# An expert's rows gathered from DRAM by an indirect DMA in place of one-hot matmuls

## The chip, the cores and the metric

The kernel runs on one core of one Trainium2 chip. The metric is the device time of one execution in microseconds, lower is better. TensorE (PE) multiplies, VectorE (DVE) and ScalarE (ACT) do elementwise work, GpSimd (POOL) has a queue of its own for transfers, and SyncE (SP) issues the weight transfers. All transfers of the core share its 16 DMA engines.

## What is computed

A two-layer encoder on 256 tokens of 1024 channels in float32. Each layer adds a mixer (attention, Fourier and recurrent branches) and a feed-forward block. The block of the second layer is the one that matters here, a mixture of 8 experts of which each token uses 2:

```
logits = xt @ w_router                      # (256, 8)
top_v, top_i = top_k(logits, 2)
top_w = softmax(top_v)
comb = sum(one_hot(top_i, 8) * top_w[..., None], axis=1)
for e in range(8):
    y = y + comb[:, e:e+1] * swiglu(xt, w_gu[e], w_down[e])
```

`xt` is the normalized input of the block. The expert widths are 1024 to 2 x 1536 and 1536 to 1024.

## The kernel before

**Precision.** Matmuls on fp32r operands stand in for float32 ones: each operand is split into a high part (`_hi`, an ACT copy that rounds) and a low part (`_lo`, a DVE subtraction), and three matmuls (high x high, high x low, low x high; L1245 to L1247) make one product.

**Weights.** They come in units of 128 x 1024 floats (512 KB). SP issues one transfer for each, and in the experts a ring of 18 units is filled ahead: unit u is issued when DVE has split unit u-18. ACT (L456) and DVE (L758) split each unit into a ring of four, and ACT may start unit u only when PE has used unit u-4. In the code of ACT and DVE, step k of a turn splits unit k, three ahead of PE (`AHEAD = 3`).

**An expert's turn.** The loop runs over the 8 experts, 36 units each. Only the tokens routed to an expert are computed: up to 128 slots, which is one tile. A second pass `experts(1)` for more than 128 tokens stands behind a condition and is not executed with these inputs. DVE builds `g_t`, a one-hot matrix of tokens against slots (`build_g`, L1078). PE multiplies it by the normalized activations, which were split once into `yhf` and `ylf` (`gather`, L1470 and L1471: 8 matmuls of 128x512). ACT and DVE copy the two halves of the result from PSUM into `xrow` (L654, L1105). PE transposes `xrow` (`turn_rows`, L1481: 8 transposes), and ACT and DVE split the result into `xg_h` and `xg_l` (L659, L1110), on which the gate and up matmuls of the next turn run. So the rows of expert e+1 are gathered within turn e, between units 24 and 25, and turned between units 27 and 28. The results of an expert are put back by `scatter` (L1491, L1492) with the transposed one-hot matrix `gt_t`, and DVE adds them to `h` (L1124).

**PE's order in a turn:** gate and up units 0 to 7, `scatter` of the last expert, units 8 to 15 with `turn_product(0)` (L1556) between, transposes of `g_t` and a matmul for the slots' weights (L1577, L1579), down units 16 to 19, `turn_product(1)`, gate and up units 20 to 24, `gather`, units 25 to 27, `turn_rows`, down units 28 and 29, `turn_product(2)`, 30 to 35.

**Ahead of the turns.** After the norm (L769), PE transposes the activations (L1306). ACT and DVE copy the result (L683, L1130) and split the normalized rows (L679, L1135, and L435 on POOL). The router's matmuls (L1501) and a chain of small DVE steps (L1189 to L1207) give each token's place. DVE builds the first `g_t`; PE gathers and turns the first rows. `keep_warm(n)` (L1295) is n transposes whose result nobody reads.

**The table `cst`** holds constants; **`hn`** is the part of `gates` that holds the normalized rows.

Of the kernel before, what the change touches and what calls it, by code (L numbers as in the profile page):

```python
# [8 lines left out]
F32 = mybir.dt.float32  # L9
F32R = mybir.dt.float32r  # L10
# [56 lines left out]
NA = len(UNITS_ATT)  # L67


C_ID, C_TRI, C_ONE, C_IOTA, C_CC, C_MASK, C_DFT, C_I8 = 0, 128, 256, 384, 640, 896, 960, 1472  # L70
C_COLS = 1480
FIRST_SLOTS = 128


def constants():

    c = np.zeros((P, C_COLS), np.float32)
    i = np.arange(P)
    c[:, C_ID:C_ID + P] = np.eye(P)
    c[:, C_TRI:C_TRI + P] = i[:, None] < i[None, :]  # L80
    c[:, C_ONE:C_ONE + P] = 1.0
    c[:, C_IOTA:C_IOTA + P] = np.where(i < FIRST_SLOTS, i, -1)
    c[:, C_IOTA + P:C_IOTA + 2 * P] = FIRST_SLOTS + i
# [16 lines left out]
    c[:, C_I8:C_I8 + 8] = np.arange(8)  # L100
    return c


def build(nc, x, norm_mix_g, w_in, b_in, rpb, conv_w, conv_b, lru_wa, lru_ba, lru_wx, lru_bx,
# [12 lines left out]
    with ExitStack() as ctx:  # L117
# [3 lines left out]
        def sem(name):  # L121
# [43 lines left out]
        gt_t = sb("gt_t", [P, TT, P], F32R)  # L165
        idx = sb("idx", [P, TT, 8], U32)
        cnt_i = sb("cnt_i", [P, 2], I32)
        eps_t = sb("eps_t", [P, 1])
        ps = ctx.enter_context(nc.psum_tensor("ps", [P, 8, 512], F32))

# [68 lines left out]
        hnh_ok, hnl_dve, hnl_pool, xt_a, xt_d, lg_ps, lg_row, lg_t, lg_d, w2_ok, mask_ok, comb_ok, pos_ps, cnt_ps, cnt_ok = (  # L239
            sem("hnh_ok"), sem("hnl_dve"), sem("hnl_pool"), sem("xt_a"), sem("xt_d"), sem("lg_ps"), sem("lg_row"), sem("lg_t"), sem("lg_d"), sem("w2_ok"), sem("mask_ok"), sem("comb_ok"), sem("pos_ps"),  # L240
            sem("cnt_ps"), sem("cnt_ok"))
        g_ok, gr_ps, xr_a, xr_d, gth_ps, xgh_ok, xgl_ok, gt_ps, gt_ok, slot_zero, ysh_ok, ysl_ok, sc_ps, sc_add = (
            sem("g_ok"), sem("gr_ps"), sem("xr_a"), sem("xr_d"), sem("gth_ps"), sem("xgh_ok"), sem("xgl_ok"), sem("gt_ps"), sem("gt_ok"), sem("slot_zero"),
            sem("ysh_ok"), sem("ysl_ok"), sem("sc_ps"), sem("sc_add"))
# [160 lines left out]
        def _(pool):  # L405
# [25 lines left out]
            mixer(1)  # L431
            load_row(final_g, 0, normed, 2 * TT * 4)

            pool.wait_ge(hnh_ok, 1)
            pool.tensor_tensor(ylf[:, 0:D], gflat[:, 0:D], yhf[:, 0:D].bitcast(F32),  # L435
                               ALU.subtract).then_inc(hnl_pool, 1)


        @block.scalar
        def _(act):  # L440
# [203 lines left out]
            def experts(p):  # L644
# [29 lines left out]

                if p == 0:

                    for t in range(TT):
                        act.wait_ge(normed, 2 * (TT * 3 + t + 1))
                        act.activation(yhf[:, D * t:D * t + D], gflat[:, D * t:D * t + D], ACT.Copy).then_inc(hnh_ok, 1)  # L679
                        if t == 0:  # L680
                            for b in range(2):
                                act.wait_ge(xt_ps, 4 * 3 + b + 1)
                                act.activation(xt_full[:, 512 * b:512 * b + 512], ps[:, 4 + b, :],  # L683
                                               ACT.Copy).then_inc(xt_a, 1)
# [6 lines left out]
                else:  # L691
                    for k in range(AHEAD):
# [3 lines left out]
                gather_rows((E + 1) * p, 0)  # L696
                gather_hi((E + 1) * p, 0)
                act.wait_ge(slot_zero, p + 1)
                def turn(e, last):

                    rows_hi((E + 1) * p + 1, e)
                    for k in range(AHEAD, U_EX + AHEAD):
                        if k < U_EX or not last:
                            hi(B, k, e, U_EX)
                        if k == 4 + AHEAD:
                            silu(e, 0)
                        if k == 11 + AHEAD:
                            product_hi(e, 0)
                        if k == 12 + AHEAD:
                            silu(e, 1)  # L710
                        if k == 16 + AHEAD:
                            act.wait_ge(gt_ps, e + (E * p + 1))
                            act.activation(gt_t[:, :, :].rearrange("p t s -> p (t s)"), ps[:, 6, 0:2 * P], ACT.Copy)\
                               .then_inc(gt_ok, 1)
                            act.activation(slot_w, ps[:, 6, 2 * P:2 * P + 1], ACT.Copy).then_inc(gt_ok, 1)
                        if k == 20 + AHEAD:
                            product_hi(e, 1)
                        if k == 24 + AHEAD:
                            silu(e, 2)
                        if k == 25 + AHEAD:  # L720
# [24 lines left out]
        def _(dve):  # L745
# [337 lines left out]
            def experts(p):  # L1083
# [13 lines left out]
                def product_lo(s, e):  # L1097
# [29 lines left out]
                if p == 0:  # L1127
                    for b in range(2):
# [9 lines left out]
                    route()  # L1138
                build_g(p, 0)
                if p == 0:  # L1140
                    route_weights()
# [4 lines left out]
                gather_rows((E + 1) * p, 0)  # L1146
                gather_lo((E + 1) * p, 0)
                def turn(e, last):

                    rows_lo((E + 1) * p + 1, e)  # L1150
                    for k in range(AHEAD, U_EX + AHEAD):
# [23 lines left out]
                        if k == 33:  # L1175
                            product_lo(2, e)
# [63 lines left out]
        def _(pe):  # L1240
# [192 lines left out]
            def dense():  # L1433
# [27 lines left out]
                    down(B + 28, 2, False, False, i, 12)  # L1461
                down(B + U_FF - 4, FF_STEPS, False, True, c=BC)

            def gather(n, e):

                pe.wait_ge(g_ok, e + n)
                for half in range(2):
                    for t in range(TT):
                        o = D * t + 512 * half
# [1 line left out]
                        ins = mm(ps[:, 6 + half, :], g_t[:, t, :], ylf[:, o:o + 512], start=False, stop=(t == TT - 1))  # L1471
                    ins.then_inc(gr_ps, 1)

            def turn_rows(n, e):

                for c in range(KC):
                    if c == 0:
                        pe.wait_ge(xr_a, e + n)
                    if c == KC // 2:
# [38 lines left out]
            def experts(p):  # L1518
                B = BASE_MOE + p * E * U_EX
                n0 = (E + 1) * p  # L1520
                if p == 0:
                    pe.wait_ge(hnl_dve, 1)
                    pe.wait_ge(hnl_pool, 1)
                    keep_warm(5)
                gather(n0 + 1, 0)
                if p == 0:
                    keep_warm(3)
                turn_rows(n0 + 1, 0)
                if p == 0:
                    keep_warm(6)  # L1530

# [36 lines left out]
                with pe.Fori(0, E) as e:  # L1568
# [64 lines left out]
```

## Time and profile before

| | |
|---|---|
| median of three runs | 1172.76 us (1170.49 to 1172.87) |
| the profiled execution | 1171.27 us, with a span of 1169.5 us from the first instruction to the last |
| mean granted TensorE clock | 0.991 |
| TensorE busy | 1133.6 us, 97% of the span |
| VectorE busy | 877.4 us, 75% |
| ScalarE busy | 720.5 us, 62% |
| GpSimd busy | 24.9 us, 2% |
| DMA | 271.70 MB, mean 232 GB/s |

A row of a group of instructions gives line, engine, operation, the tiles written and read, shapes and count, then busy time and the mean of one in ns, then idle time of the engine before them. Matmuls overlap, so the distance from one start to the next, and not the duration of one, is what a matmul costs PE. The granted clock is 1.00 at 2.4 GHz, and 0.5 stands for the lower level, 1.2 GHz. The DMA share is the busy share of the 16 engines; transfers that overlap in an engine bring it a little over 1.

### The profile page before, as it was taken

The numbers are of one execution on the slowest core, as the hardware profiler recorded it, in microseconds if no ns is written. First come the engines' busy times: TensorE is split into PE (matmuls) and PEld (weight loads), VectorE is DVE, ScalarE is ACT, GpSimd is POOL, SyncE is SP. The second block draws the span as 40 slices with busy tenths as digits, with TensorE's granted clock in tenths as the row PEclk, the third lists the DMA queues.
The fourth block names the chain that finished last, engine by engine and source line by source line (L and its number), as shares of the span: only waits on it lengthen the run. The fifth ranks groups of instructions, "written<-read, shape, count | busy, mean of one in ns | idle before, by whom it ended". The sixth has DMA issues, their size and how long they took to land.

```text
span 1169.5 us, 19502 instructions
## 1 busy us (share of the span) xinstructions
PE 1133.6 (97%) x7004; PEld 996.7 (85%) x7004; DVE 877.4 (75%) x1049; ACT 720.5 (62%) x941; POOL 24.9 (2%) x21
## 2 busy tenths in 40 slices
PE   7999999989999998999999989999999999999995
PEld 7989899889999997989899868888888888888883
DVE  5976876755445456765886779999999999998995
ACT  5476764454443445376764457778787877777773
POOL 0200000000000001200000000000000000000000
PEclk9999999999999999999999999999999999999998
DMA  9954455646555567655445398999999999999940
GB/s 291 261 178 148 126 168 167 205 147 190 187 183 178 165 211 206 189 158 158 136 151 174 112 374 301 343 331 330 341 327 341 326 342 325 344 326 345 329 139 38
DMA packets 137897, 271.70 MB, mean 232 GB/s; under 512 B 26424, under 2 KB 26736, under 8 KB 137840
## 3 DMA queue, kind: packets, MB, share of 16 engines
q1 hardware_dynamic: 136832, 267.26, 69.4%
q0 software_dynamic: 1008, 3.67, 0.9%
q8 instruction: 37, 0.61, 0.2%
q14 instruction: 20, 0.16, 0.1%
HBM read 269.84 MB, written 1.05 MB: 232 GB/s over the span
## 4 chain that ended last, share of the span: by engine, by line
PE 82%; DVE 9%; ACT 5%; issue 3%; DMA 1%; DVEq 0%; ACTq 0%; POOLq 0%
PE ps L1245 25%; PE ps L1247 24%; PE ps L1246 24%; DVE w_lo L758 4%; ACT w_hi L456 2%; DVE h L1124 2%; PE ps L1358 1%; PE ps L1306 1%; PE ps L1491 1%; PE ps L1492 1%; PE ps L1471 1%; PE ps L1470 1%; PE ps L1386 1%; PE ps L1332 1%; PE ps L1481 1%
## 5 line engine op out<-in xcount | busy, mean ns | idle before, releaser
L758 DVE TENSOR_TENSOR w_lo<-raw,w_hi 128x1024 fp32r<-128x1024 f32 x304 | 370.3, 1232 | 177.6 <-ACT w_hi L456 172.7
L456 ACT ACTIVATE w_hi<-raw 128x1024 fp32r<-128x1024 f32 x304 | 318.0, 1060 | 218.0 <-PE ps L1247 208.1
L1245 PE MATMUL ps<-xh,w_hi 128*128 128x256 f32 x1024 | 292.3, 285 | 0.4 <-DVE xl L779 0.4
L1247 PE MATMUL ps<-xh,w_lo 128*128 128x256 f32 x1024 | 289.7, 283 | 0.0
L1246 PE MATMUL ps<-xl,w_hi 128*128 128x256 f32 x1024 | 289.7, 283 | 0.0
L758 DVE TENSOR_TENSOR w_lo<-mix,w_hi 128x1024 fp32r<-128x1024 f32 x192 | 230.4, 1220 | 29.1 <-ACT w_hi L456 24.0
L456 ACT ACTIVATE w_hi<-mix 128x1024 fp32r<-128x1024 f32 x192 | 203.7, 1061 | 71.9 <-PE ps L1247 71.9
L1245 PE MATMUL ps<-w_hi,xh 128*128 128x512 f32 x512 | 203.3, 397 | 0.8 <-issue 0.2
L1247 PE MATMUL ps<-w_hi,xl 128*128 128x512 f32 x512 | 199.8, 390 | 0.0
L1246 PE MATMUL ps<-w_lo,xh 128*128 128x512 f32 x512 | 199.4, 389 | 0.0
L1245 PEld LDWEIGHTS ps<-xh,w_hi 128*128 128x128 f32 x1024 | 196.4, 192 | 3.1 <-issue 2.1
L1246 PEld LDWEIGHTS ps<-xl,w_hi 128*128 128x128 f32 x1024 | 196.4, 192 | 0.3
L1247 PEld LDWEIGHTS ps<-xh,w_lo 128*128 128x128 f32 x1024 | 196.3, 192 | 0.0
L1245 PEld LDWEIGHTS ps<-w_hi,xh 128*128 128x128 f32 x512 | 96.3, 188 | 26.0 <-DVE w_lo L758 5.9
L1245 PE MATMUL ps<-w_hi,yh 128*128 128x512 f32 x288 | 115.4, 401 | 0.8
L1247 PEld LDWEIGHTS ps<-w_hi,xl 128*128 128x128 f32 x512 | 96.1, 188 | 20.8
L1247 PE MATMUL ps<-w_hi,yl 128*128 128x512 f32 x288 | 112.5, 391 | 0.0
L1246 PEld LDWEIGHTS ps<-w_lo,xh 128*128 128x128 f32 x512 | 96.3, 188 | 18.9
L1246 PE MATMUL ps<-w_lo,yh 128*128 128x512 f32 x288 | 112.3, 390 | 0.0
L1245 PEld LDWEIGHTS ps<-w_hi,yh 128*128 128x128 f32 x288 | 54.1, 188 | 14.2 <-issue 4.1
L1247 PEld LDWEIGHTS ps<-w_hi,yl 128*128 128x128 f32 x288 | 54.1, 188 | 11.8
L1246 PEld LDWEIGHTS ps<-w_lo,yh 128*128 128x128 f32 x288 | 54.2, 188 | 10.2
(202 smaller groups left out, 1126.6 us busy)
## 6 DMA issues: line engine op xcount, KB each, us to landing
mix<-in_moe_w_gu_dram SPq DMA_DIRECT2D x112, 512.0 KB, 5.2
raw<-in_w_in_dram SPq DMA_DIRECT2D x96, 512.0 KB, 4.2
raw<-in_moe_w_gu_dram SPq DMA_DIRECT2D x80, 512.0 KB, 5.6
mix<-in_moe_w_down_dram SPq DMA_DIRECT2D x80, 512.0 KB, 4.6
raw<-in_ffn_w_gu_dram SPq DMA_DIRECT2D x48, 512.0 KB, 3.8
raw<-in_w_branch_dram SPq DMA_DIRECT2D x24, 512.0 KB, 3.4
raw<-in_ffn_w_down_dram SPq DMA_DIRECT2D x24, 512.0 KB, 4.7
raw<-in_w_out_dram SPq DMA_DIRECT2D x16, 512.0 KB, 3.4
```

The source lines that it names most:

```text
L456: act.activation(w_hi[:, u % RH, :], src, ACT.Copy).then_inc(hi_done, 1)
L758: dve.tensor_tensor(w_lo[:, u % RH, :], place(u)[0], w_hi[:, u % RH, :].bitcast(F32), ALU.subtract).then_inc(lo_done, 1)
L1124: dve.tensor_tensor(h[:, t, 512 * half:512 * half + 512], ps[:, (6, 7, 4, 5)[q], :], h[:, t, 512 * half:512 * half + 512], ALU.add).then_i ...
L1245: mm(dst, ah, bh, start=first, stop=False, skip_group_check=True)
L1246: mm(dst, ah, bl, start=False, stop=False, skip_group_check=True)
L1247: return mm(dst, al, bh, start=False, stop=last, skip_group_check=True)
L1306: ins = pe.transpose(ps[:, 4 + c // 2, at:at + P], hn[:, t, P * c:P * c + P], ident)
L1332: ins = mm(ps[:, 4 + m, 0:SEQ], uf_t[:, BR * t + P * m:BR * t + P * m + P], cst[:, at:at + SEQ], start=(t == 0), stop=(t == TT - 1))
L1358: ins = mm(ps[q, 4 + 2 * g + m // 2, SEQ * (m % 2):SEQ * (m % 2) + SEQ], wlru[q, d, g, m, :], conv_t[q, m, :], start=True, stop=True)
L1386: ins = mm(ps[HD * hh:HD * hh + HD, 6, P * t:P * t + P], v_t[:, kt, HD * hd:HD * hd + HD], pt_t[:, hh, P * kt:P * kt + P], start=(kt == 0) ...
L1470: mm(ps[:, 6 + half, :], g_t[:, t, :], yhf[:, o:o + 512], start=(t == 0), stop=False)
L1471: ins = mm(ps[:, 6 + half, :], g_t[:, t, :], ylf[:, o:o + 512], start=False, stop=(t == TT - 1))
```

## The change

The normalized rows are written once to a DRAM tensor `hn_rows` (two POOL transfers of 512 KB). For each expert PE multiplies `g_t` by the tokens' numbers (`token_id`, two equal columns), which gives the row number of each slot; DVE casts one column to `slot_row`, and POOL issues an indirect DMA that fetches row `slot_row[p]` of `hn_rows` into partition p of `xrow` (128 rows of 4 KB). Empty slots fetch row 0. In the first pass the splits of the normalized rows, the one-hot matmuls and the two copies into `xrow` are gone. In the second pass, which isn't executed, they stand as before. On PE the row numbers are computed between units 23 and 24, and the rows are turned between units 29 and 30. `build_g` moves from step 23 to step 21 of DVE, `gather_hi` and `gather_lo` from steps 31 to 32.

```
# POOL
-            pool.wait_ge(hnh_ok, 1)
-            pool.tensor_tensor(ylf[:, 0:D], gflat[:, 0:D], yhf[:, 0:D].bitcast(F32),
-                               ALU.subtract).then_inc(hnl_pool, 1)
+            for t in range(TT):
+                pool.wait_ge(normed, 2 * (TT * 3 + t + 1))
+                pool.dma_start(hn_rows[P * t:P * t + P, :], hn[:, t, :]).then_inc(rows_out, 16)
+
+            def gather_rows():
+
+                pool.indirect_dma_start(xrow, None, hn_rows, bass.IndirectOffsetOnAxis(slot_row[:, 0:1], 0)).then_inc(xr_in, 16)
+
+            pool.wait_ge(rows_out, 16 * TT)
+            pool.wait_ge(row_ok, 1)
+            gather_rows()
+            for e in range(E):
+
+                pool.wait_ge(row_ok, e + 2)
+                pool.wait_ge(gth_ps, 2 * e + 2)
+                gather_rows()
# ACT, ahead of the turns: the copies of hn into yhf go; in a turn gather_rows only if p
-                    for t in range(TT):
-                        act.wait_ge(normed, 2 * (TT * 3 + t + 1))
-                        act.activation(yhf[:, D * t:D * t + D], gflat[:, D * t:D * t + D], ACT.Copy).then_inc(hnh_ok, 1)
...
-                        if k == 25 + AHEAD:
-                            gather_rows((E + 1) * p + 1, e)
-                        if k == 28 + AHEAD:
+                        if p and k == 25 + AHEAD:
+                            gather_rows(1, e)
+                        if k == 29 + AHEAD:
                             gather_hi((E + 1) * p + 1, e)
# DVE
+                def rows_of_slots(n, e=0):
+                    dve.wait_ge(row_ps, e + (n + 1))
+                    dve.tensor_copy(slot_row[:, :], ps[:, 7, 0:1]).then_inc(row_ok, 1)
...
-                    dve.wait_ge(hnh_ok, 2)
-                    dve.tensor_tensor(ylf[:, D:2 * D], gflat[:, D:2 * D], yhf[:, D:2 * D].bitcast(F32),
-                                      ALU.subtract).then_inc(hnl_dve, 1)
...
-                        if k == 23:
+                        if k == 21:
 
                             dve.wait_ge(gt_ps, e + (E * p + 1))
                             build_g(p, e + 1)
+                        if k == 23:
                             product_lo(1, e)
-                        if k == 28:
-                            gather_rows((E + 1) * p + 1, e)
-                        if k == 31:
+                        if p == 0 and k == 26:
+                            rows_of_slots(1, e)
+                        if p and k == 28:
+                            gather_rows(1, e)
+                        if k == 32:
                             gather_lo((E + 1) * p + 1, e)
# PE
+            def rows_of_slots(n, e):
+
+                pe.wait_ge(g_ok, e + n)
+                for t in range(TT):
+                    ins = mm(ps[:, 7, 0:2], g_t[:, t, :], token_id[:, t, :], start=(t == 0), stop=(t == TT - 1))
+                ins.then_inc(row_ps, 1)
...
-            def turn_rows(n, e):
-
+            def turn_rows(n, e, p):
+
+                if p == 0:
+                    pe.wait_ge(xr_in, e * 16 + 16 * n)
...
                 if p == 0:
-                    pe.wait_ge(hnl_dve, 1)
-                    pe.wait_ge(hnl_pool, 1)
-                    keep_warm(5)
-                gather(n0 + 1, 0)
-                if p == 0:
-                    keep_warm(3)
-                turn_rows(n0 + 1, 0)
+                    pe.wait_ge(token_ok, 1)
+                    rows_of_slots(1, 0)
+                    keep_warm(20)
+                else:
+                    pe.wait_ge(hnl_dve, TT)
+                    gather(1, 0)
+                turn_rows(1, 0, p)
...
-                    gate_up(20, 2, e, range(5))
+                    gate_up(20, 2, e, range(4))
                     pe.wait_ge(gt_ok, e * 2 + 2 * (E * p + 1))
-                    gather(n0 + 2, e)
-                    gate_up(20, 2, e, range(5, 8))
-                    turn_rows(n0 + 2, e)
+                    if p:
+                        gather(2, e)
+                    else:
+                        rows_of_slots(2, e)
+                    gate_up(20, 2, e, range(4, 8))
                     down(28, 1, e, range(2))
+                    turn_rows(2, e, p)
                     turn_product(2, e)
```

## Rows read from the trace of the kernel before

**Rows 1.** The page: busy time of each engine.
```profile
PE 1133.6 (97%) x7004; PEld 996.7 (85%) x7004; DVE 877.4 (75%) x1049; ACT 720.5 (62%) x941; POOL 24.9 (2%) x21
```

**Rows 2.** Stretches (a turn; its dense part): PE, PEld, DVE, ACT, POOL, clock, DMA share, GB/s.
```profile
882.40:939.10 56.70, 56.53 (x260) 45.95 (x259) 51.99 (x53) 43.49 (x49) 0.00 (x0) 1.00 0.96 333
905.00:913.50 8.50, 8.50 (x43) 7.08 (x42) 6.67 (x7) 5.98 (x7) 0.00 (x0) 1.00 1.02 373
```

**Rows 3.** Who waited for whom, 769.0 to 1109.1 us (six turns).
```profile
ACT w_hi L456 <- PE ps L1247: 77.4, 174, 2.2
DVE w_lo L758 <- ACT w_hi L456: 21.2, 26, 1.4
PEld ps L1245 <- DVE w_lo L758: 4.4, 12, 0.5
```

**Rows 4.** PE in order of time, one turn: last matmul of unit 23 to turn_rows.
```profile
904.86 0.39 PE L1247 MATMUL ps<-w_hi,xl 128*128 128x512 f32 x1
...
906.45 0.39 PE L1470 MATMUL ps<-yh,g_t 128*128 128x512 f32 x1
...
908.32 0.40 PE L1245 MATMUL ps<-w_hi,xh 128*128 128x512 f32 x1
...
912.43 1.03 PE L1481 MATMUL ps<-cst,gates 128*128 128x128 f32 x8
```

**Rows 5.** PE in order of time: small matmuls in a turn and in the router.
```profile
893.21 0.50 PE L1579 MATMUL ps<-small,g_t 128*128 x4
...
691.34 0.37 PE L1514 MATMUL ps<-small,cst 128*128 128x8 f32 x2
691.56 0.37 PE L1515 MATMUL ps<-small,cst 128*128 128x8 f32 x2
```

**Rows 6.** DVE in order of time, the same turn, and the cast nearest to slot_row.
```profile
902.72 4.90 DVE L758 TENSOR_TENSOR w_lo<-mix,w_hi 128x1024 fp32r<-128x1024 f32 x4
...
911.00 2.59 DVE L758 TENSOR_TENSOR w_lo<-mix,w_hi 128x1024 fp32r<-128x1024 f32 x2 [1.35 <-ACT w_hi L456]
...
691.75 0.17 DVE L1207 COPY small<-ps 128x16 f32<-128x16 f32 x1 [0.85 <-PE ps L1514]
```

**Rows 7.** DMA issues of stretches at 242, 522, 682, 905 us, and of the page: us to landing.
```profile
row<-in_norm_mix_g_dram POOLq DMA_DIRECT2D x1, 512.0 KB, 3.6
...
row<-in_norm_ffn_g_dram POOLq DMA_DIRECT2D x1, 512.0 KB, 7.1
raw<-in_w_in_dram SPq DMA_DIRECT2D x1, 512.0 KB, 6.8
...
row<-in_final_g_dram POOLq DMA_DIRECT2D x1, 512.0 KB, 8.0
...
mix<-in_moe_w_gu_dram SPq DMA_DIRECT2D x5, 512.0 KB, 5.0
...
raw<-in_w_branch_dram SPq DMA_DIRECT2D x24, 512.0 KB, 3.4
```

**Rows 8.** POOL's queue in the microsecond from 686.2: packets, MB, share of 16 engines.
```profile
q0 software_dynamic: 60, 0.25, 62.5%
```

**Rows 9.** Stretches ahead of the turns (columns as in Rows 2).
```profile
676.60:679.70 3.10, 0.59 (x3) 0.17 (x1) 2.75 (x6) 2.42 (x5) 0.00 (x0) 1.00 1.02 385
679.70:683.30 3.60, 3.53 (x17) 3.08 (x18) 2.52 (x6) 2.64 (x6) 1.08 (x2) 0.53 1.04 391
...
700.00:704.00 4.00, 4.00 (x19) 3.31 (x18) 3.90 (x5) 3.53 (x5) 0.00 (x0) 1.00 0.30 57
```

**Rows 10.** Ahead of the turns in order of time: POOL, ACT, DVE, PE.
```profile
682.20 0.53 POOL L410 DMA_DIRECT2D row<-in_final_g_dram  x1 [158.99 <-DVE gates L769]
...
683.06 1.06 ACT L679 ACTIVATE yh<-gates 128x1024 fp32r<-128x1024 f32 x1
...
691.96 0.60 DVE L1078 TENSOR_SCALAR g_t<-cst,small 128x128 fp32r<-128x128 f32 x2
...
698.22 0.48 PE L1245 MATMUL ps<-w_hi,xh 128*128 128x512 f32 x1
```

More of the change, by code:

```diff
@@ L67 @@
 NA = len(UNITS_ATT)
-C_ID, C_TRI, C_ONE, C_IOTA, C_CC, C_MASK, C_DFT, C_I8 = 0, 128, 256, 384, 640, 896, 960, 1472
-C_COLS = 1480
+C_ID, C_TRI, C_ONE, C_IOTA, C_CC, C_MASK, C_DFT, C_I8, C_TOK = 0, 128, 256, 384, 640, 896, 960, 1472, 1480
+C_COLS = 1484
 FIRST_SLOTS = 128
@@ L100, in constants @@
     c[:, C_I8:C_I8 + 8] = np.arange(8)
+    for t in range(TT):
+        c[:, C_TOK + 2 * t:C_TOK + 2 * t + 2] = (t * P + i)[:, None]
     return c
@@ L167, in build @@
         cnt_i = sb("cnt_i", [P, 2], I32)
+        token_id = sb("token_id", [P, TT, 2], F32R)
+        slot_row = sb("slot_row", [P, 1], U32)
+        hn_rows = nc.dram_tensor("hn_rows", (SEQ, D), F32, kind="Internal").ap()
         eps_t = sb("eps_t", [P, 1])
@@ L237, in build @@
         silu_ok, prod_ok, ah_ok, al_ok, at_ps = sem("silu_ok"), sem("prod_ok"), sem("ah_ok"), sem("al_ok"), sem("at_ps")
-        hnh_ok, hnl_dve, hnl_pool, xt_a, xt_d, lg_ps, lg_row, lg_t, lg_d, w2_ok, mask_ok, comb_ok, pos_ps, cnt_ps, cnt_ok = (
-            sem("hnh_ok"), sem("hnl_dve"), sem("hnl_pool"), sem("xt_a"), sem("xt_d"), sem("lg_ps"), sem("lg_row"), sem("lg_t"), sem("lg_d"), sem("w2_ok"), sem("mask_ok"), sem("comb_ok"), sem("pos_ps"),
+        hnh_ok, hnl_dve, xt_a, xt_d, lg_ps, lg_row, lg_t, lg_d, w2_ok, mask_ok, comb_ok, pos_ps, cnt_ps, cnt_ok = (
+            sem("hnh_ok"), sem("hnl_dve"), sem("xt_a"), sem("xt_d"), sem("lg_ps"), sem("lg_row"), sem("lg_t"), sem("lg_d"), sem("w2_ok"), sem("mask_ok"), sem("comb_ok"), sem("pos_ps"),
             sem("cnt_ps"), sem("cnt_ok"))
+        rows_out, token_ok, row_ps, row_ok, xr_in = sem("rows_out"), sem("token_ok"), sem("row_ps"), sem("row_ok"), sem("xr_in")
         g_ok, gr_ps, xr_a, xr_d, gth_ps, xgh_ok, xgl_ok, gt_ps, gt_ok, slot_zero, ysh_ok, ysl_ok, sc_ps, sc_add = (
@@ L675, in experts @@
                 if p == 0:
-                    for t in range(TT):
-                        act.wait_ge(normed, 2 * (TT * 3 + t + 1))
-                        act.activation(yhf[:, D * t:D * t + D], gflat[:, D * t:D * t + D], ACT.Copy).then_inc(hnh_ok, 1)
[L680 to L684, printed above, removed]
+                    for b in range(2):
+                        act.wait_ge(xt_ps, 4 * 3 + b + 1)
+                        act.activation(xt_full[:, 512 * b:512 * b + 512], ps[:, 4 + b, :], ACT.Copy).then_inc(xt_a, 1)
                     link(act.activation(table_in, eps_t[:, 0:1], ACT.Exp))
@@ L691, in experts @@
                 else:
+                    for t in range(TT):
+                        act.activation(yhf[:, D * t:D * t + D], gflat[:, D * t:D * t + D], ACT.Copy).then_inc(hnh_ok, 1)
                     for k in range(AHEAD):
@@ L695, in experts @@
                     link(act.activation(table_in, eps_t[:, 0:1], ACT.Silu))
-                gather_rows((E + 1) * p, 0)
+                else:
+                    gather_rows(0, 0)
                 gather_hi((E + 1) * p, 0)
@@ L1133, in experts @@
                     link(dve.memset(gt_t[:, :, :].bitcast(F32), 0.0))
-                    dve.wait_ge(hnh_ok, 2)
-                    dve.tensor_tensor(ylf[:, D:2 * D], gflat[:, D:2 * D], yhf[:, D:2 * D].bitcast(F32),
-                                      ALU.subtract).then_inc(hnl_dve, 1)
+                    dve.tensor_copy(token_id[:, :, :], cst[:, C_TOK:C_TOK + 2 * TT].rearrange("p (t a) -> p t a", t=TT))\
+                        .then_inc(token_ok, 1)
                     lo(B, 0)
                     route()
+                else:
+                    for t in range(TT):
+                        dve.wait_ge(hnh_ok, t + 1)
+                        dve.tensor_tensor(ylf[:, D * t:D * t + D], gflat[:, D * t:D * t + D],
+                                          yhf[:, D * t:D * t + D].bitcast(F32), ALU.subtract).then_inc(hnl_dve, 1)
                 build_g(p, 0)
                 if p == 0:
+                    rows_of_slots(0)
                     route_weights()
@@ L1145, in experts @@
                     lo(B, k)
-                gather_rows((E + 1) * p, 0)
+                if p:
+                    gather_rows(0, 0)
                 gather_lo((E + 1) * p, 0)
@@ L1462, in dense @@
                 down(B + U_FF - 4, FF_STEPS, False, True, c=BC)
+            def rows_of_slots(n, e):
+                pe.wait_ge(g_ok, e + n)
+                for t in range(TT):
+                    ins = mm(ps[:, 7, 0:2], g_t[:, t, :], token_id[:, t, :], start=(t == 0), stop=(t == TT - 1))
+                ins.then_inc(row_ps, 1)
             def gather(n, e):
-                pe.wait_ge(g_ok, e + n)
+                pe.wait_ge(g_ok, e + (E + 1 + n))
                 for half in range(2):
@@ L1472, in gather @@
                     ins.then_inc(gr_ps, 1)
-            def turn_rows(n, e):
+            def turn_rows(n, e, p):
+                if p == 0:
+                    pe.wait_ge(xr_in, e * 16 + 16 * n)
                 for c in range(KC):
-                    if c == 0:
+                    if p and c == 0:
                         pe.wait_ge(xr_a, e + n)
-                    if c == KC // 2:
+                    if p and c == KC // 2:
                         pe.wait_ge(xr_d, e + n)
@@ L1583, in experts @@
                     turn_product(1, e)
-                    gate_up(20, 2, e, range(5))
+                    gate_up(20, 2, e, range(4))
                     pe.wait_ge(gt_ok, e * 2 + 2 * (E * p + 1))
-                    gather(n0 + 2, e)
-                    gate_up(20, 2, e, range(5, 8))
-                    turn_rows(n0 + 2, e)
+                    if p:
+                        gather(2, e)
+                    else:
+                        rows_of_slots(2, e)
+                    gate_up(20, 2, e, range(4, 8))
                     down(28, 1, e, range(2))
+                    turn_rows(2, e, p)
                     turn_product(2, e)
```

1 line of the change is left out of this document (added).

## The prediction

> **What bounds the kernel now.** I read the page first, then the table of stretches, then the waits, then single turns in order of time. PE is busy for 97% of the span, DVE for 75% [rows 1]. A turn of an expert takes 56.7 us; in it PE is busy 56.53, DVE 51.99 and ACT 43.49 us at a DMA share of 0.96 and 333 GB/s [rows 2]. So three resources are close together, and the waits tell which of them leads. Over six turns ACT waited 77.4 us for PE to free a slot of the weight ring, DVE waited 21.2 us for ACT, and PE waited 4.4 us for DVE [rows 3]. PE sets the pace and pulls the others behind it. The weights come 18 units ahead. With 391 GB/s seen ahead of the turns [rows 9], a turn's 18.9 MB need 48 us, so DMA has slack on the average. It has none in the dense part, with a share of 1.02 at 373 GB/s [rows 2].
>
> **Part 1: what leaves a turn.** From the first gather matmul at 906.45 to unit 25 at 908.32 are 1.87 us [rows 4]. PE has no wait there, so this is its full price. DVE loses one copy of 128x512 from PSUM, and ACT another, some 0.7 us each by the width of a split of twice the size [rows 6]. Neither leads; I count them at nothing. PE covers them, and if that cover were gone they would be worth at most 0.7 us a turn.
>
> **Part 2: what PE gets.** Two matmuls of two columns. No row shows that shape. The nearest are four small ones in a turn, 0.50 us in all (0.25 for two), and the router's, 0.22 us from one pair to the next, which would be 0.45 for two that overlapped no better than those pairs [rows 5]. I take 0.40, near the upper end because the weight loads of `g_t` are alone there. The net gain of PE is 1.87 - 0.40 = 1.47 us a turn, 11.8 us in eight.
>
> **Part 3: the new wait in a turn.** PE waits for `xr_in` ahead of `turn_rows`. Everything is queued behind that on PE, so a late transfer costs its full lateness. Call X the start of unit 23's last matmul, 904.86 in the turn of [rows 4]. The row numbers' second matmul starts at about X+0.4, and 0.41 us pass between such a matmul and the DVE step on it (691.34 to 691.75 [rows 5, 6]), so DVE could cast at X+0.84. But the cast stands behind the split of unit 26. DVE did four splits in 4.90 us from 902.72 [rows 6]; the third of them, unit 26, ended at about 906.4, X+1.5. With 0.17 for the cast and 0.15 for the semaphore POOL issues at X+1.85. PE meanwhile starts unit 24 at X+0.63. Three units take 908.32 to 912.43, 1.37 us each [rows 4]; six of them bring it to `turn_rows` at X+8.8. So the transfer is hidden if it lands within L = 8.8 - 1.85 - 0.1 = 6.85 us of its issue.
>
> **How long is L?** No indirect DMA is in the trace. The nearest are POOL's row loads, also 512 KB in 4 KB pieces: 3.6 us on idle DMA engines, 7.1 where SP's load took 6.8, and 8.0 in the flood of loads ahead of the turns [rows 7]. At moderate load the extra over an idle engine is the same on both queues: 7.1 - 3.6 = 3.5 for POOL, and 6.8 - 3.4 = 3.4 for SP, whose shortest median is 3.4 [rows 7]. In the dense part of a turn SP's loads land in 5.0 us [rows 7], an extra of 1.6. So a direct load of POOL would take about 5.2. The indirect one adds the reading of 128 numbers and their addresses, for which I take 0.5 to 1.5 us on the 0.53 of a direct issue [rows 10]; no row bounds it. Its own 0.5 MB, and the denser PE (18.9 MB a turn become 19.4), lengthen the queue by perhaps 0.5. That makes 6.2 to 7.2 and up to 8.0 + 1.5 = 9.5 if the queue is as full as in the flood; the lower end is 5.2. I take 7.0, near to the row with SP at 5.0, that is 0.15 to 0.2 us of stall. In the last turn no weights are left to load and L is near 4. Stalls: 7 x 0.2 = 1.4 us.
>
> A rule can be weighed against this. The rows show 3.6 us for 512 KB on an idle queue and 8.0 on a full one [rows 7]. The Trainium skill, "DMA: Bandwidth & Descriptors", section "Anatomy of one DMA", gives about 2.0 us plus the bytes over 436e3 per us, 3.2 us here; by it the new wait would never be seen in a turn, nor would most of part 4, and the sum would be rival D's. The trace agrees only for the idle queue.
>
> **Part 4: ahead of the turns.** The rows must be in DRAM before the first gather. POOL issues the two writes behind the load of `final_g`, which it issues at 682.20 [rows 10], all in the flood (share 1.02 and 1.04, and 0.30 from 700 on [rows 9]). That load moved 0.25 MB in the microsecond from 686.2 [rows 8], 4.0 us behind its issue, and I take 686 for its first packets. Three transfers of 0.52 MB then end at 686 + 6.3 = 692.3, and with 1.5 us for the last bytes' landing the rows are out at about 694. The row numbers are ready earlier: the first `g_t` at 692.5 [rows 10], less 1.06 us since ACT's second copy no longer stands ahead of the table load and the first split, plus about 0.7 for matmul and cast: 692.1. So the writes lead, and ACT's gain is hidden by them. The gather issued at 694 takes the flood's 8.0 us (the flood ends at 700 [rows 9], with 1 MB of writes about 702.7): the rows are in at 702. Transposes, ACT's split and DVE's take about 2.0 us to unit 0 (the half turn 0.4, ACT 0.6, DVE 0.7, semaphores): 704.0 against 698.22 [rows 10], 5.8 us late. PE is idle from the end of `keep_warm(20)` at about 694 to 702. After a gap of 2.6 us the clock was granted at 0.53 for 3.6 us (679.7 to 683.3) [rows 9]; here unit 0 starts 2 us into such a stretch, which costs half of 1.6 us, plus 0.2 on the transposes: 1.0. Total 6.8 us. Bounds: rows out at 692.5 and 7.2 us of landing give 699.7 and +4.0; 696 and 9.0 give 705 and +10. The removed first gather (2 us) and copies are inside this reckoning, since it is from unit 0 to unit 0.
>
> **The sum.** -11.8 + 1.4 + 6.8 = -3.6 us. The profiled execution took 1171.27 (span 1169.5 and 1.8 around it), 1.5 under the median of 1172.76. I put the difference on the median: 1172.76 - 3.6 = 1169.2.
>
> **Rivals.** B, slower: **the gather lands late in every turn.** Its place is the wait ahead of `turn_rows`; its price is 7 x (L - 6.85). It turns the sign of the sum at L = 7.56 (7 x 0.71 = 5.0 = 11.8 - 6.8) and shows as slower from 7.9. At L = 8.5: -11.8 + 11.6 + 6.8 = +6.6, 1179.4. For it: 7.1 and 8.0 on busy engines [rows 7]. Against it: SP's 5.0 in a turn.
> C: **VectorE becomes the bound.** It is busy 51.99 of 56.7 us; its wait of 1.35 us behind the gather [rows 6] goes. If its order allows no further closing up, a turn gains only its own 0.5 us: -4.0 + 6.8 = +2.8, 1175.6. Against it: PE would still need 55.2 us, 3.8 more than DVE.
> D: **the start costs nothing**, because transfers of POOL are served sooner: unit 0 at about 698, -11.8 + 1 = 1162. Against it are the packets of [rows 8].
> E: **POOL's descriptor work is held up by DVE**, whose splits are nearly back to back, 1.22 us each [rows 6]. One such split on L gives 8.2 - 6.85 = 1.3 a turn in the worst case and half of it on the average: 7 x 0.8 = 5.6, so +0.6, 1173.4. The Trainium skill, "SBUF — State Buffer", section "Who interferes with whom", says that a VectorE instruction with two SBUF inputs contends with a GpSimd instruction that reads SBUF; no row here shows a POOL issue beside such splits in a turn.
> The change does what it says: the 9 gathers before all belong to the first pass, and the second isn't executed.
>
> **How the numbers follow.** Forecast 0.50, B 0.22, C 0.10, D 0.06, E 0.12. A measurement of this kernel can tell about 0.2%, 2.3 us. With 6.8 uncertain by 2.5 the forecast is faster in 0.42 and no change in 0.08; B gives slower 0.17 and same 0.05; C 0.06 and 0.04; D faster 0.06; E same 0.10 and slower 0.02. That is faster 0.48, same 0.27, slower 0.25. The range reaches from near D, 1163.5, to B at L = 8.5, 1179.0, which leaves out some 0.15 to 0.2. The forecast's own range is 1165.5 to 1172.
>
> **What would show it.** A turn of 55.3 to 55.5 us; PE's wait at L1481 for the DMA of `xrow` under 0.3 us a turn; a landing of 6 to 7 us for the indirect transfer; a cast about 1.7 us behind unit 23's last matmul; unit 0 of the first turn at about 704 with a PE gap of 8 us and a low clock before it. Wrong would be: turns near 56.7 with a long wait for `xrow` (B), waits of PE for `w_lo` grown (C), unit 0 near 698 (D), or POOL instructions of over 2 us (E).

## The result, and the profile after

The changed kernel took 1176.39 us (1175.38 to 1178.84 in seven runs), the one before 1172.3 us (1170.49 to 1173.29 in seven) on the same chip. The ratio is 1.0040 [1.0028, 1.0051]: slower by about 4 us. Later, against other runs of before, it was 1.0049 [1.0035, 1.0063]. The forecast was 1169.2, faster by 3.6. Its range, to 1179.0, held the time.

The profiled execution took 1178.02 us, with a span of 1176.1. The page, with the busy time of each engine, and the chain that ended last, by engine:

```profile
PE 1121.3 (95%) x6962; PEld 987.1 (84%) x6962; DVE 874.0 (74%) x1049; ACT 713.8 (61%) x930; POOL 37.9 (3%) x31
...
PE 72%; DVE 10%; DMA 7%; ACT 6%; issue 4%; DVEq 0%; POOL 0%; SPq 0%; ACTq 0%
```

PE has 12.3 us less work than in [rows 1], and the kernel is no faster for it: PE now waits. Who it waited for, over six turns (as in [rows 3]: total, times, longest):

```profile
ACT w_hi L475 <- PE ps L1277: 67.0, 161, 2.2
DVE w_lo L775 <- ACT w_hi L475: 15.3, 24, 1.4
PEld ps L1275 <- DVE w_lo L775: 9.4, 18, 0.9
PEld ps L1520 <- DMA gates<-hn_rows,slot_row: 8.2, 6, 1.6
...
PE ps L1275 <- DVE yl L1117: 2.6, 6, 0.5
```

The fourth line is the new wait, for the gathered rows (L1520 is `turn_rows`): 8.2 us over six turns, with the weight load that stands ahead of the transposes. The third line has grown from 4.4, and the last one is new. Then one turn in order of time, first PE, then DVE's cast with the split behind it, then POOL, then the landing as the chain of waits has it:

```profile
914.92 0.28 PE L1498 MATMUL ps<-token_id,g_t 128*128 128x2 f32 x2
...
924.24 0.98 PE L1520 MATMUL ps<-cst,gates 128*128 128x128 f32 x7 [0.77 <-DMA gates<-hn_rows,slot_row]
...
928.96 0.49 PE L1275 MATMUL ps<-w_hi,yh 128*128 128x512 f32 x1 [0.42 <-DVE yl L1117]
...
915.99 0.15 DVE L1122 CAST slot_row<-ps 128x1 uint32<-128x1 f32 x1
916.22 1.23 DVE L775 TENSOR_TENSOR w_lo<-mix,w_hi 128x1024 fp32r<-128x1024 f32 x1
...
916.41 1.84 POOL L446 DMA_INDIRECT gates<-hn_rows,slot_row  x1 [54.54 <-DVE slot_row L1122]
...
916.41 7.78 DMA gates<-hn_rows,slot_row
```

Unit 23's last matmul starts at 914.69, so that is X. POOL issues at X+1.72. PE would reach the transposes at X+8.6 (unit 24 starts at 915.06, and six units of 1.37 us follow), but the rows land at 924.19, 7.78 us behind their issue. The stretch of this turn, and its dense part (columns as in [rows 2]):

```profile
882.40:938.80 56.40, 55.11 (x254) 44.79 (x253) 51.67 (x54) 43.14 (x49) 1.84 (x1) 1.00 0.96 344
912.00:920.00 8.00, 8.00 (x38) 6.66 (x37) 7.14 (x8) 6.43 (x8) 1.84 (x1) 1.00 1.05 388
```

A turn takes 56.4 us. It was 56.7 [rows 2], and the prediction named 55.3 to 55.5 as the sign of being right. The start, in order of time (the router's first matmul, the first landing of rows, unit 0), with POOL's instructions:

```profile
686.17 3.62 PE L1540 MATMUL ps<-gates,rw 128*8 128x256 f32 x16
...
705.50 1.97 PE L1520 MATMUL ps<-cst,gates 128*128 128x128 f32 x8 [7.20 <-DMA gates<-hn_rows,slot_row]
...
708.40 0.78 PE L1275 MATMUL ps<-w_hi,xh 128*128 128x512 f32 x1
...
685.07 0.53 POOL L416 DMA_DIRECT2D row<-in_final_g_dram  x1 [158.98 <-DVE gates L786]
685.59 1.06 POOL L442 DMA_DIRECT2D hn_rows<-gates  x2
697.13 1.85 POOL L446 DMA_INDIRECT gates<-hn_rows,slot_row  x1 [10.48 <-DMA hn_rows<-gates]
```

Everything up to the router is 2.9 us later in this execution: its first matmul (L1501 before) stood at 683.26. That stretch comes ahead of the change, and why it was longer was not tested. It is no peculiarity of this execution: in the eleven traces with the change or a variant of it this matmul stands between 684.7 and 687.2, and of the kernel before there is one trace, whose time is 1.0 us below its median. So whether some of this difference belongs to the change is not shown. I count from the router's first matmul. From there to unit 0 it was 14.96 us and is now 22.23, 7.3 more (21.5 to 22.4 in the four other traces with this start and an indirect gather). The clock behind the wait costs about 0.7 besides: from unit 0 to the first turn's transposes it takes 46.02 us here and 45.35 with the one-hot start of experiment 2, each less PE's wait for the rows. From unit 0 to the end it was 471.28 and is 467.70, 3.6 less. Together +3.7, and the medians say +4.1.

### The profile page after: what moved, and what is told of

It is laid out like the page before. It is cut to its first block, busy times and chain, and to the rows that moved or that the text cites. A ratio compares the mean times of both kernels' runs of the same rounds, so it can differ in the third digit from the quotient of the medians.

```text
span 1176.1 us, 19440 instructions
## 1 busy us (share of the span) xinstructions
PE 1121.3 (95%) x6962; PEld 987.1 (84%) x6962; DVE 874.0 (74%) x1049; ACT 713.8 (61%) x930; POOL 37.9 (3%) x31
## 4 chain that ended last, share of the span: by engine, by line
PE 72%; DVE 10%; DMA 7%; ACT 6%; issue 4%; DVEq 0%; POOL 0%; SPq 0%; ACTq 0%
PE ps L1275 22%; PE ps L1277 22%; PE ps L1276 22%; DMA gates<-hn_rows,slot_row 5%; DVE w_lo L775 4%; ACT w_hi L475 3%; DVE h L1145 2%; PE ps L1388 1%; DMA hn_rows<-gates 1%; PE ps L1530 1%; DVE gates L786 1%; DMA h<-in_x_dram 1%; PE ps L1531 1%; PE ps L1416 1%; DVE yl L1117 1%
## 5 line engine op out<-in xcount | busy, mean ns | idle before, releaser
L1275 PEld LDWEIGHTS ps<-w_hi,yh 128*128 128x128 f32 x288 | 54.1, 188 | 17.2 <-DVE w_lo L775 6.8
L1277 PEld LDWEIGHTS ps<-w_hi,yl 128*128 128x128 f32 x288 | 54.1, 188 | 11.6
```

The lines of the kernel that those rows point to most:

```text
L1275: mm(dst, ah, bh, start=first, stop=False, skip_group_check=True)
L1277: return mm(dst, al, bh, start=False, stop=last, skip_group_check=True)
```

## The experiments

Theory, after the result: two places each give back what PE gained. T, the turn: the rows land about 1 us later than they are hidden for. S, the start: the rows' way through DRAM costs 7 to 8 us that the one-hot matmuls don't. Rivals: V, VectorE had become the bound; and POOL's long issue or the `final_g` load as the true causes of T and S. Each diff is against the changed kernel; a0_after is that kernel again, run beside experiments 5, 6 and e7_first_early.

**1. The rows sooner (T against V).** Row numbers, `build_g` and the cast two units earlier, the transposes where they are.

```
-                        if k == 21:
+                        if k == 19:
                             build_g(p, e + 1)
...
-                        if p == 0 and k == 26:
+                        if p == 0 and k == 24:
                             rows_of_slots(1, e)
...
-                    gate_up(20, 2, e, range(4))
+                    gate_up(20, 2, e, range(2))
...
-                    gate_up(20, 2, e, range(4, 8))
+                    gate_up(20, 2, e, range(2, 8))
```

> The row numbers are computed two units earlier (PE between units 21 and 22, DVE builds the one-hot matrix at step 19 and casts at step 24), all else as in the changed kernel. Theory L (the transfer is 1.1 us too late in seven turns): the cover grows by two units, 2.7 us, to about 9.6 us against a landing of 7.9, so PE's wait for the rows goes to 0, a turn falls from 56.4 to about 55.2 us and the time by 7 to 10 us, to 1167-1169. Rival V (VectorE's order sets the turn, the wait for the rows only stands where another wait would): the turn stays above 56.1 us, PE's waits for w_lo grow by what the wait for the rows loses, time 1174-1176.

1168.26 us, a ratio to before of 0.9965 [0.9954, 0.9977]. A turn, and what PE still waited for over six turns:

```profile
882.00:937.28 55.28, 54.76 (x254) 44.74 (x253) 51.49 (x54) 42.90 (x49) 1.87 (x1) 1.00 0.98 351
...
PEld ps L1275 <- DVE w_lo L775: 9.4, 18, 0.9
```

The wait for the rows is gone in every turn, and the turn fell to 55.28 us. DVE has the same work, and PE's wait for its splits stayed at 9.4 us. So T holds and V falls: that wait comes with the denser order and is in the 55.28 already. The landings, 7.7 to 9.4 us, were no shorter; they had 2.7 us more cover.

**2. The first rows by one-hot matmuls (S).** Ahead of the turns all stands as in the kernel before; the turns gather by DMA.

```
+                    keep_warm(5)
                     gather(1, 0)
+                    keep_warm(3)
...
-                if p == 0:
-                    pe.wait_ge(xr_in, e * 16 + 16 * n)
+                if p == 0 and n == 2:
+                    pe.wait_ge(xr_in, e * 16 + 16)
```

> Only the first expert's rows are made by one-hot matmuls as in the kernel before (with the splits, copies and keep_warm calls that this needs); the rows of the other turns are still gathered by the indirect DMA. Theory S (the start costs about 7.3 us plus 0.5 to 1 of a low clock): unit 0 of the first turn stands 16 us behind the end of the router's matmuls again instead of 22-23, time 1176.4 - 8 = 1168-1169. Rival (the cost is in the turns alone, the start is paid back there since the loads get ahead): 1174-1176.

1169.38 us, 0.9968 [0.9956, 0.9979]. Unit 0 stood at 701.16 and the router's first matmul at 686.20: 14.96 us, to the hundredth what it was before. S holds, with 8.4 us by the ratios (7.3 and some 0.7 of clock are the 8.0 of the traces).

**3. The writes ahead of `final_g` (is it the queue?).**

```
-            load_row(final_g, 0, normed, 2 * TT * 4)
...
             gather_rows()
+            load_row(final_g, 0, normed, 2 * TT * 4)
```

> The two writes of the normalized rows are issued as soon as each tile is there and ahead of the load of final_g, which goes behind the first gather. Theory S with POOL's queue served in order: the writes start 1.9 us earlier and 0.52 MB less stands ahead of them (2.1 us), so rows out, first gather and unit 0 come 3.5 to 4.5 us earlier, time 1172-1173. Rival (the landing of the writes is set by the flood of weight loads, not by what stands ahead of them on their queue): only the 1.9 us of the earlier issue, 1174.5.

1176.13 us, 1.0033 [1.0023, 1.0044]: a miss. POOL and PE in order of time:

```profile
694.89 1.00 POOL L444 DMA_INDIRECT gates<-hn_rows,slot_row  x1 [10.49 <-DVE slot_row L1121]
...
702.39 1.97 PE L1519 MATMUL ps<-cst,gates 128*128 128x128 f32 x8 [6.25 <-DMA gates<-hn_rows,slot_row]
```

The writes landed in 8.1 us in place of 10.1, and now POOL waited for the cast of `slot_row`: the index chain, which the prediction had ready only 2 us before the writes were out, came last. The writes were out at 692.13, the cast ended at 694.07. From the router to unit 0 it was 20.27 us, 2 us shorter than in the profiled execution of after, while the medians show only 0.3. The same edit on top of the early rows (e7_first_early):

> e3_writes_first and e1_early together. Theory: the start 1.5-2.5 us shorter than in e1_early, turns of 55.3 us: 1166-1167. If the medians of e3 against the changed kernel (no gain) hold, 1168.

1167.87 us, 0.9959 [0.9945, 0.9973], 0.4 us below the early rows alone. Both differences are within their intervals, though both traces have the shorter start (20.27 and 20.72 us, where the five with the old order of POOL's queue have 21.5 to 22.4). Whether this order gives anything in the time stays open; most of S is not the place in the queue.

**4. A plain load in place of the indirect one (what is L made of?).** POOL loads rows 0 to 127 for every expert, with the same bytes, wait and trigger. The experts then compute on the wrong rows: this leaves out the gather itself, and serves to price it.

```
-                pool.indirect_dma_start(xrow, None, hn_rows, bass.IndirectOffsetOnAxis(slot_row[:, 0:1], 0)).then_inc(xr_in, 16)
+                pool.dma_start(xrow, hn_rows[0:P, :]).then_inc(xr_in, 16)
```

> Every indirect DMA is a direct load of rows 0 to 127 into the same tile, at the same place; the row numbers are computed and cast but not used, so every expert computes on the wrong rows. It prices the indirect form by itself. Theory I (the indirect form costs 1.3 us more descriptor work, 1.84 against 0.53, and the rest of the landing is the queue of weight loads): landing 6.5-6.8 in a turn, PE's wait about 0 to 0.1, a turn of 55.3, time 1168-1169.5. Rival Q (the queue of the DMA engines alone sets when the packets start, and the descriptor work is hidden in it): landing stays at 7.7-8, time 1176. My prediction's step had 5.2 for a direct load.

1166.73 us, 0.9946 [0.9932, 0.9961]. Turns of 55.26 us without a wait for the rows, but for 0.45 us in the first, where they landed in 7.4. The page, median of nine landings, and the last turn, where no weights are left to load:

```profile
gates<-hn_rows POOLq DMA_DIRECT2D x9, 512.0 KB, 6.6
...
gates<-hn_rows POOLq DMA_DIRECT2D x1, 512.0 KB, 3.4
```

The answers for the indirect one in the kernel after: the page's median, and the last turn.

```profile
gates<-hn_rows,slot_row POOLq DMA_INDIRECT x9, 7.9
...
gates<-hn_rows,slot_row POOLq DMA_INDIRECT x1, 4.4
```

So the load on the DMA engines makes 3.4 into 6.6, and the indirect form adds 1.0 on idle engines and 1.3 in a turn. The 1.3 is the longer POOL instruction, 1.84 us for 0.53: from the end of the instruction to the landing it takes 6.0 us for the direct load and 6.1 for the indirect one (medians of the seven turns under load).

The same trace has SP's weight loads beside POOL's. The first line below is of two that SP issued 2.9 and 1.6 us ahead of POOL's load at 912.88, the second of two that it issued 0.2 ahead of it and 1.2 behind, the third is POOL's:

```profile
mix<-in_moe_w_gu_dram SPq DMA_DIRECT2D x2, 512.0 KB, 4.9
...
mix<-in_moe_w_gu_dram SPq DMA_DIRECT2D x2, 512.0 KB, 6.4
gates<-hn_rows POOLq DMA_DIRECT2D x1, 512.0 KB, 6.3
```

Under the same load the two queues take the same time, and POOL's 512 KB make both longer: over six turns the medians are 5.3 us for the SP load 1.6 us ahead, 6.5 for the one 0.2 ahead, and 6.5 for POOL's.

**5. One unit later (the slope).** Row numbers one unit later, cast at step 27.

```
-                        if p == 0 and k == 26:
+                        if p == 0 and k == 27:
...
-                    gate_up(20, 2, e, range(4))
+                    gate_up(20, 2, e, range(5))
```

> The row numbers are computed one unit later than in the changed kernel (PE between units 24 and 25, cast at step 27). Theory L (each us less of cover is a us more of stall in seven turns): PE's wait per turn grows by 1.37 us, a turn from 56.4 to 57.7, time 1176.4 + 9.5 = 1185-1187; the last turn, where nothing is loaded any more, stays without a stall. Rival V (VectorE's order sets the turn): under 1179.

1189.41 us, 1.015 [1.0135, 1.0166]; a0_after in the same set had 1177.82. That is 11.6 us more where 9.5 were expected. For a0_after itself this had been expected:

> The changed kernel itself again, on the same chip as the others of this set, so that small differences are read against it: 1.003-1.005 of the kernel before, PE's wait for the rows 0.9-1.2 us in each of the seven turns under load, transfers landing in 7.8-8.0 us.

Its ratio of 1.0049 is as expected. Its landings, 7.3 to 8.8 us, and PE's waits for the rows, 0.3 to 1.8 us, spread wider than that.

In experiment 5 the wait over six turns grew to 15.5 us by the line below. The transposes of two turns follow, and then the stretches right behind them:

```profile
PEld ps L1520 <- DMA gates<-hn_rows,slot_row: 15.5, 6, 2.7
...
871.03 1.97 PE L1520 MATMUL ps<-cst,gates 128*128 128x128 f32 x8 [2.25 <-DMA gates<-hn_rows,slot_row]
...
929.74 1.09 PE L1520 MATMUL ps<-cst,gates 128*128 128x128 f32 x8 [2.25 <-DMA gates<-hn_rows,slot_row]
...
871.00:875.00 4.00, 3.97 (x17) 3.72 (x18) 1.77 (x3) 2.56 (x4) 0.00 (x0) 0.57 1.02 378
...
929.75:933.75 4.00, 4.00 (x24) 3.42 (x24) 2.55 (x4) 3.32 (x5) 0.00 (x0) 1.00 1.03 377
```

Four turns took 57.5 to 58.0 us and three 58.6 to 58.7. The two gaps are equal, and yet the granted clock was 0.57 for 4 us behind the one and 1.00 behind the other. Over the seven turns it was 0.57 behind gaps of 2.25, 2.25 and 2.20 us and 1.00 behind gaps of 2.25, 2.15, 2.14 and 1.96, so the length of the gap alone does not tell. The later rows cost 7 x 1.3 = 9.1 us, near to the 9.5, and the low clock some 3 more (three turns, 0.95 us each), 12 in all against the 11.6 measured.

**6. Both repairs.** The one-hot start and the early rows together.

> The one-hot start of e2_onehot_start and the earlier row numbers of e1_early together. Theory S+L (two costs at two places that add): about 7 us under each of the two, 1161-1163, turns of 55.3 us without a wait for the rows, 0.991 of the kernel before. Rival (they share a bound, as each alone came to 1168-1169): 1166-1168.

1161.07 us, 0.9904 [0.9891, 0.9918]: by the ratio 11.3 us faster than before, and 16.8 faster than the changed kernel beside it (a0_after). By the ratios, the early rows alone gave 8.8 and the one-hot start alone 8.4, in all 17.2. The two costs are separate and add up, and this version beats both kernels.

**7. The cast ahead of a DVE step with one SBUF input (why 1.84 us?).** `product_lo(1)` moves from step 23 to right behind the cast.

```
-                        if k == 23:
-                            product_lo(1, e)
                         if p == 0 and k == 26:
                             rows_of_slots(1, e)
+                        if k == 26:
+                            product_lo(1, e)
```

> DVE's subtraction of the second product (a 128x512 step with one input in PSUM and one in SBUF, 0.68 us) is moved from step 23 to right behind the cast of the row numbers, so that the indirect DMA is issued beside it and not beside a split, whose two inputs are both in SBUF. No work is added or left out. Theory D (the descriptor work cannot start until the running split ends, as the issues of 1.84 us beside a split and of 0.94-1.00 us without one suggest): POOL's instruction falls from 1.84 to 0.95-1.0 us, the landing from 7.9 to 7.0, PE's wait by 0.9 us a turn, time 6 us under the changed kernel, 1170-1171. Rival Q (the load on the DMA engines lengthens the descriptor work): still 1.84 us and no gain.

1170.21 us, 0.9971 [0.996, 0.9983]. POOL and DVE in order of time, the wait over six turns, and a turn:

```profile
914.74 0.94 POOL L446 DMA_INDIRECT gates<-hn_rows,slot_row  x1 [54.33 <-DVE slot_row L1122]
...
914.38 0.68 DVE L1117 TENSOR_TENSOR yl<-ps,yh 128x512 fp32r<-128x512 f32 x1
...
PEld ps L1520 <- DMA gates<-hn_rows,slot_row: 0.7, 3, 0.3
...
882.40:937.68 55.28, 54.76 (x254) 44.68 (x253) 51.37 (x54) 43.00 (x49) 0.94 (x1) 1.00 0.98 351
```

The instruction took 0.94 us in place of 1.84, at the same DMA load, and the rows landed in 6.3 to 6.9 (7.3 in the first turn, with 0.3 us of wait). What DVE runs behind the cast is thus worth 0.9 us of issue and at least as much of landing, a full turn's stall. At 6.8 to 6.9 the weight load waits for 0.2 to 0.3 us and at 6.6 and below not at all, so the threshold of 6.85 was about right.

**8. The weight loads held back (the load).** SP issues no weights past unit 5 of an expert until its rows are in; its loop over the experts is written out for that.

```
-                with sp.Fori(0, E) as e:
+                for e in range(E):
...
+                                    if p == 0 and k == 6:
+                                        sp.wait_ge(xr_in, 16 * (e + 1))
```

> SP holds its weight loads before unit 6 of each expert until the rows of that expert have landed, so that the DMA engines are nearly empty when the indirect DMA is issued, in the turns and ahead of them; SP's loop over the experts is written out. Theory Q (of the landing of 7.9 us some 3 us are the weight loads queued ahead): the landing falls to 5.3 us in the turns (4.4 plus the 0.9 of a split) and to about 4.5-5.5 at the start, PE's wait for the rows goes to 0, the writes of the normalized rows land in 3-5 us instead of 10. Whether the time falls depends on the loads: a turn's 48 us of them plus some 7 us of pause are about the turn itself, so 1160 if they still arrive in time, above 1180 with waits for weights if not. Rival (the indirect form is slow by itself under any load): the landing stays above 7.

1164.81 us, 0.9935 [0.9917, 0.9954]. The stretch of a gather:

```profile
907.09:910.09 3.00, 3.00 (x15) 2.49 (x14) 2.50 (x3) 2.38 (x3) 1.84 (x1) 1.00 0.19 34
```

The rows landed in 4.2 us at the start and in 4.9 to 5.4 in the second to the seventh turn, where PE did not wait for them. In the first turn the engines were full all the same: the share was 1.05, the rows landed in 7.95 us, and PE waited. Perhaps the loads held back at the start were still being caught up; that was not tested.

```profile
740.15:743.15 3.00, 3.00 (x15) 2.49 (x14) 2.50 (x3) 2.38 (x3) 1.87 (x1) 1.00 1.05 388
...
748.14 1.09 PE L1522 MATMUL ps<-cst,gates 128*128 128x128 f32 x8 [0.93 <-DMA gates<-hn_rows,slot_row]
```

So one trace holds both cases, with the same instruction of 1.84 to 1.88 us: 7.95 us at a share of 1.05, and 5.27 at 0.19. POOL's instruction still took 1.84 us at a DMA share of 0.19: the load on the DMA engines doesn't lengthen the issue, DVE does. The start took 16.98 us from the router to unit 0, 5.3 less than in the kernel after, so most of S is the flood of weight loads that meets the writes and the gather. From the second turn on, holding the weights cost PE nothing that shows (turns of 55.3 us).

## Why the prediction was wrong

**The sum, term by term.** Removed from turns: forecast 8 x 1.47 = 11.8, measured 8 x (56.7 - 55.28) = 11.4. Stalls: forecast 1.4, measured 7 x (56.4 - 55.28) = 7.8. Start: forecast 6.8, measured 7.3 and about 0.7 of clock, 8.0. That is +4.4 in place of -3.6, against +3.7 in the profiled executions and +4.1 in the medians. The stall is 6.4 of the 8.0 us between the two sums, the start 1.2, the turns 0.4.

**The step that failed is "How long is L?", and in it the 0.5 us for the gather's own bytes and the denser PE.** The forecast had L at 7.0; it was 7.9. Part 3's timing around it was right: X+1.72 for X+1.85, X+8.6 for X+8.8, and a threshold of 6.85 that experiment 7 met. Taken apart by the runs, L in a turn is 3.4 us for a direct load on idle engines (experiment 4, the last turn); 1.0 for the indirect form (4.4, the kernel after, the last turn); about 0.9 behind a running split of DVE (5.3 in the last turn of experiment 1, where the issue took 1.86); and 2.6, the rest, of queue. The rest is less than the 3.2 of the direct load (6.6 over 3.4), since of the 1.9 us that the other two add on idle engines only 1.3 show under load. The prediction took the queue at 1.6 by SP's landings of 5.0 in a turn, on the ground that both queues have the same extra over an idle engine [rows 7], and added 0.5. The ground was right: in experiment 4 SP's loads beside POOL's took 6.4 and POOL's 6.3, where each queue has 3.4 on idle engines. What was short is the 0.5. SP's landings of 5.0 in the kernel before had no gather among them. In experiment 4 they were 5.3 just ahead of it, and 6.5 beside it. That is 1.5 and not 0.5, of which 1.2 came with POOL's 512 KB (which at the 388 GB/s of this stretch are 1.35 us of transfer, an estimate). With it the direct load comes to 3.4 + 1.6 + 1.5 = 6.5, as measured, and the indirect form's 1.3 makes 7.8 to 7.9. The term was wrong by 1.0, L by 0.9.

The packets of POOL's queue in the first microsecond in which it moved more than two, 5 us behind the issue at 916.41, show where the time goes:

```profile
q0 software_dynamic: 77, 0.32, 79.8%
```

Nothing of POOL moved for 4 us (1.84 of them are the instruction), and then the whole 0.5 MB went in some two. On idle DMA engines, in the last turn, the packets began in the second microsecond behind the issue. The indirect form's extra, 1.3 us with the split, was within the 0.5 to 1.5 that I gave it. The Trainium skill, "DMA: Bandwidth & Descriptors", section "Anatomy of one DMA", has a formula by which 512 KB take an estimated 3.2 us. The trace has 3.4 for the direct load on idle engines, but 7.9 for the one that counts.

**Part 2.** The two small matmuls cost PE 0.14 us, not 0.40 (914.92, and unit 24 at 915.06). That gain of 0.26 was lost to the wait of 0.42 at 928.96 for `product_lo`, which is new and stands in the trace of every variant (in experiment 5 in four turns of six). Together they leave a turn without a stall at 55.28, where the sum had 55.23.

**Part 4.** Right in mechanism, and its rows were the right ones: the gather issued 11.5 us behind the first write (11.25 forecast), a landing of 8.3 (8.0), a PE gap with a low clock behind it. The 1.5 us that it took for the last bytes' landing had no row; the sum that it stands in came out. What was short is the step from rows to unit 0: 2.9 us and not 2.0, since the transposes ran at the lower clock (1.97 us for eight, 1.03 in [rows 4]). The stretches around it (columns as in [rows 9]):

```profile
697.00:701.00 4.00, 1.30 (x7) 0.90 (x5) 2.25 (x2) 0.00 (x0) 1.85 (x1) 0.50 1.05 405
701.00:705.40 4.40, 0.00 (x0) 0.00 (x0) 0.00 (x0) 0.00 (x0) 0.00 (x0) 0.50 1.02 405
705.40:709.00 3.60, 3.50 (x16) 3.40 (x17) 1.55 (x3) 2.09 (x4) 0.00 (x0) 0.50 0.40 150
709.00:713.00 4.00, 4.00 (x17) 3.27 (x16) 3.51 (x4) 3.12 (x4) 0.00 (x0) 0.88 0.10 11
```

ACT and DVE have almost nothing to do for 8 us while the DMA engines are full; the first turn's weights arrive that nobody can use yet.

**The rivals.** B had the place and the direction: L past the 7.56 at which the sum turned. Its 22% was too low since the 5.0 held against it came from a stretch without the gather's own bytes. E's mechanism was there, but held for 0.9 us and not a whole split: the issue ends some 0.8 us behind the running split (916.41 + 1.84 against 916.22 + 1.23). It takes a split that is already running. In the last turn of the kernel after the split began 0.08 us behind the issue, and the issue took 0.94:

```profile
1142.38 0.94 POOL L446 DMA_INDIRECT gates<-hn_rows,slot_row  x1 [54.95 <-DVE slot_row L1122]
...
1142.46 1.23 DVE L775 TENSOR_TENSOR w_lo<-mix,w_hi 128x1024 fp32r<-128x1024 f32 x1 [0.35 <-ACT w_hi L475]
```

The Trainium skill, "SBUF — State Buffer", section "Who interferes with whom", has a VectorE instruction with two SBUF inputs contend with a GpSimd instruction that reads SBUF. Experiment 7 agrees for the indirect form, 1.84 us against 0.94; the direct one of experiment 4 took 0.53 behind the same split. The queue (B) and the hold (E) were priced as rivals, each alone; both came together. With the queue alone (experiment 7) the kernel is faster than before, and so it is with the hold alone (experiment 8, which also shortens the start). C fell with experiment 1, D with the start.

## What to carry to other kernels

Price a transfer by landings under the load that it will meet, and count its own bytes into that load: here 512 KB took 3.4 us on idle engines, 6.6 under load where others without it among them took 5.0, and 7.9 as an indirect gather. Where an indirect gather takes work off the bounding engine, give it more cover than its worst landing (here 9.4 us), issue it where VectorE has not just begun a step with two SBUF inputs, and leave the first use, which has no cover, as it was. A wait that is hidden "but for 0.2 us" is one whose sign isn't known: each microsecond on it counts once for every turn.

## What the runs showed of the hardware that was not expected

- GpSimd's indirect DMA instruction (128 rows of 4 KB) took 0.93 to 1.00 us where no DVE subtraction with two SBUF inputs was running at its start, also where one began 0 to 0.25 us later. Where one had begun 0.13 to 0.26 us ahead it took 1.83 to 1.94 us, and 1.4 where it had begun 0.7 ahead, ending 0.8 to 0.9 us behind it, whatever the DMA share (0.19 or 1.05). A direct one took 0.53 in either case. This holds for each of the gathers of all traces.
- While SP's queue kept the engines at a share of 1.05, POOL's queue moved nothing for 4 us behind its issue; then it had 0.32 MB in a microsecond and SP's 0.10. SP's loads that met it landed in 6.4 us and more in place of 5.3.
- A gap of PE of 2.25 us was followed by a granted clock of 0.57 for 4 us in two turns, and by 1.00 in another of the same loop (experiment 5).
